# Sixteen conditioning units of a two-block transformer moved from TensorE's products to multiply-adds on GpSimd

## The reference

```python
c_act = jax.nn.silu(c)                                   # (1, 1024)
for l in range(2):
    if l == 1:
        kv_shift, kv_scale = split(c_act @ kv_ada_w + kv_ada_b, 2)
    sh1, sc1, g1, sh2, sc2, g2 = split(c_act @ ada_w[l] + ada_b[l], 6)
    h = x * (1 + sc1) + sh1
    out = conv_module(h) if l == 0 else moba_attention(h @ w_q, k, v) @ w_o
    x = layer_norm(ALPHA * x + (1 + g1) * out, ...)
    h = x * (1 + sc2) + sh2
    f = swiglu(h, ffn_w13, ffn_w2) if l == 0 else moe_swiglu(h, ...)
    x = layer_norm(ALPHA * x + (1 + g2) * f, ...)
return second_block(x, ...)
```

## Time and profile before

| | us |
|---|---|
| runs, median of 3 | 2249.0 (2247.69 to 2250.14) |
| profiled execution | 2244.34 |
| its span | 2242.6 |
| TensorE busy in the span | 2175.9 |
| VectorE, ScalarE, GpSimd busy | 1711.5, 1362.7, 94.1 |
| feed-forward stage, 190.0 to 388.1 | 198.1 |
| ln1, 388.1 to 404.5 | 16.4 |
| k, v, q, 404.5 to 472.5 | 68.0 |
| attention, 472.5 to 521.5 | 49.0 |

### The profile page before, as it was taken

How to read it: one execution, slowest core, us unless ns; L and a number is a source line. 1 busy time by engine, 2 the same in 40 slices (tenths; PEclk the granted TensorE clock), 3 DMA queues, 4 the chain that set the end, 5 groups by cost and what they waited for, 6 DMA issues and landing times.

```text
span 2242.6 us, 35191 instructions
## 1 busy us (share of the span) xinstructions
PE 2175.9 (97%) x14098; PEld 1846.7 (82%) x14098; DVE 1711.5 (76%) x1688; ACT 1362.7 (61%) x1266; POOL 94.1 (4%) x166
## 2 busy tenths in 40 slices
PE   7999999998999999999999999999999999999998
PEld 4767999876888888888888888888998898888887
DVE  3876445646888888888888898886677478999966
ACT  3145334545777777777777777774555335777744
POOL 7500000001000000000000000000000000000000
PEclk8999999999999999999999999999999999999999
DMA  9685754674599999999999999996951152999960
GB/s 356 237 286 183 261 188 161 233 251 163 211 350 393 385 371 370 372 370 372 368 374 369 372 365 377 370 372 182 194 163 39 34 176 76 363 368 366 370 225 20
DMA packets 294171, 619.76 MB, mean 276 GB/s; under 512 B 24845, under 2 KB 102488, under 8 KB 294008
## 3 DMA queue, kind: packets, MB, share of 16 engines
q1 hardware_dynamic: 293200, 617.18, 77.9%
q10 hardware_dynamic: 808, 0.30, 0.1%
HBM read 615.30 MB, written 1.05 MB: 275 GB/s over the span
## 4 chain that ended last, share of the span: by engine, by line
PE 90%; DVE 5%; ACT 2%; DMA 2%; issue 1%; SPq 1%; DVEq 0%; ACTq 0%
PE bank L1325 11%; PE bank L1326 11%; PE bank L1327 11%; PE bank L2291 6%; PE bank L2293 6%; PE bank L2292 6%; PE bank L1367 6%; PE bank L1366 6%; PE bank L1368 6%; PE bank L2352 2%; PE bank L1341 1%; PE bank L1402 1%; PE bank L1299 1%; PE bank L635 1%; PE bank L2491 1%; PE bank L2410 1%
## 5 line engine op out<-in xcount | busy, mean ns | idle before, releaser
L1456 DVE TENSOR_TENSOR ring_lo<-ring_raw,ring_hi 128x2048 fp32r<-128x2048 f32 x432 | 988.4, 2291 | 132.6 <-ACT ring_hi L1449 132.0
L1449 ACT ACTIVATE ring_hi<-ring_raw 128x2048 fp32r<-128x2048 f32 x432 | 828.1, 1920 | 294.4 <-PE bank L1327 174.6
L1325 PE MATMUL bank<-ring_hi,xg_hi 128*128 128x512 f32 x1152 | 456.8, 397 | 1.9 <-DVE ring_lo L1456 1.9
L1326 PE MATMUL bank<-ring_hi,xg_lo 128*128 128x512 f32 x1152 | 449.6, 390 | 0.0
L1327 PE MATMUL bank<-ring_lo,xg_hi 128*128 128x512 f32 x1152 | 449.4, 390 | 0.0
L507 DVE TENSOR_TENSOR ring_lo<-ring_raw,ring_hi 128x2048 fp32r<-128x2048 f32 x95 | 215.8, 2280 | 119.2 <-ACT ring_hi L489 106.0
L2291 PE MATMUL bank<-Hh,ring_hi 128*128 128x256 f32 x936 | 266.4, 285 | 2.7 <-DVE ring_lo L507 1.4
L2293 PE MATMUL bank<-Hh,ring_lo 128*128 128x256 f32 x936 | 264.9, 283 | 0.0
L2292 PE MATMUL bank<-Hl,ring_hi 128*128 128x256 f32 x904 | 255.8, 283 | 0.0
L1327 PEld LDWEIGHTS bank<-ring_lo,xg_hi 128*128 128x128 f32 x1152 | 216.2, 188 | 46.8
L1325 PEld LDWEIGHTS bank<-ring_hi,xg_hi 128*128 128x128 f32 x1152 | 216.4, 188 | 46.6 <-issue 2.7
(11 more groups left out here) (542 smaller groups left out, 2730.2 us busy)
## 6 DMA issues: line engine op xcount, KB each, us to landing
ring_raw<-in_moe_w SPq DMA_DIRECT2D x672, 512.0 KB, 5.2
ring_raw<-in_ada_w SPq DMA_DIRECT2D x96, 512.0 KB, 5.2
ring_raw<-in_ffn_w SPq DMA_DIRECT2D x66, 512.0 KB, 4.8
ring_raw<-in_exp_gate SPq DMA_DIRECT2D x64, 512.0 KB, 5.2
ring_raw<-in_exp_up SPq DMA_DIRECT2D x64, 512.0 KB, 5.3
ring_raw<-in_exp_down SPq DMA_DIRECT2D x64, 512.0 KB, 5.3
ring_raw<-in_w_in SPq DMA_DIRECT2D x42, 512.0 KB, 7.4
ring_raw<-in_conv_in_w SPq DMA_DIRECT2D x16, 512.0 KB, 9.3
```

The costliest lines, as they stand in the source:

```text
L1325: mm(o, xg_hi[:, g, kk, :], wh(k), start=(kk == 0), stop=False)
L1326: mm(o, xg_lo[:, g, kk, :], wh(k), start=False, stop=False)
L1449: nc.scalar.activation(ring_hi[:, at % SPLIT, :], ring_raw[:, n % RAW, :], ACT.Copy)\
L1456: nc.vector.tensor_tensor(ring_lo[:, at % SPLIT, :], ring_raw[:, n % RAW, :], ring_hi[:, at % SPLIT, :].bitcast(F32), ALU.subtract).then_i ...
```

## The change

Four of the six vectors of the second layer (1.0, 1.2, 1.3, 1.4; sixteen units) are no longer multiplied by TensorE. GpSimd multiplies each raw unit, in its slot, by the value of `c_act` that belongs to each partition (`TENSOR_SCALAR`), and adds the result to a sum of 128x1024 in SBUF (`TENSOR_TENSOR`). TensorE then adds over the partitions and turns in one step: `turn_sum`, eight products of a 128x128 block of the sum with a column of ones. The row copies on ScalarE go. The sixteen units are spread over the list: one behind each ffn2, k and v unit until there are no more, which is one behind each of ffn2 0 to 10, k 0 to 3 and v 0. SyncE waits for GpSimd's mark "added n" before it reuses such a slot, and the count `unit_done` leaves them out. In attention, `turn_sum` stands at heads 1, 5 and 9 and three keep-warm products at the odd heads 7, 11, 13 and 15. The calls of `split_hi` and `split_lo` are put in terms of split units (`two_ahead`); those of the code quoted above stay.

```diff
-    late = [("ada", 1, j) for j in range(4)]
+    SUMMED = (0, 2, 3, 4)
+    summed_parts = [("ada", 1, 4 * v + i) for v in SUMMED for i in range(4)]
+    late = list(summed_parts)
+
+    def summed_part():
+        if late:
+            ada_part(1, late.pop(0)[2], A["ada_w"][1])
 
     def down(j):
         add(("ffn2", j), w2, 0, D, 2, r0=256 * j)
-        for _ in range(3):
-            if late:
-                key = late.pop(0)
-                ada_part(1, key[2], A["ada_w"][1])
+        summed_part()
...
     for j in range(4):
         add(("k", j), A["w_kv"], 256 * j)
+        summed_part()
     for j in range(4):
         add(("v", j), A["w_kv"], D + 512 * (j // 2), 512, 4, r0=512 * (j % 2))
+        summed_part()
     for j in range(4):
         add(("q", j), A["w_q"][0], 256 * j)
-    ada(1, 2, 5)
+    assert not late
...
+                elif m in on_pool:
+                    sp.eng.wait_ge(*T.at("added %d" % m))
                 else:
                     sp.eng.wait_ge(T.sem("unit_done"), done_at(m))
...
+            pool.eng.wait_ge(*T.at("ccol"))
+            pool.eng.wait_ge(*T.at("mm mean ln0"))
+            for _, l, j in summed_parts:
+                n = at_unit[("ada", l, j)]
+                w, _ = weights(n)
+                total = sum_of[j // 4]
+                landed(pool, n)
+                for k in range(2):
+                    kk = 2 * (j % 4) + k
+                    eng.tensor_scalar(w[:, k, :] if kk else total, w[:, k, :], cpad[:, kk, 0:1], None, ALU.mult)\
+                        .then_inc(pool.tick(f"added {n}"), 1)
+                for k in range(2):
+                    if 2 * (j % 4) + k:
+                        pool.eng.wait_ge(*pool.own())
+                        eng.tensor_tensor(total, total, w[:, k, :], ALU.add).then_inc(pool.tick(f"added {n}"), 1)
+                T.mark(f"sum {l} {j // 4}", *pool.last)
...
-                for _ in range(3):
-                    if late:
-                        adaptive(1, late.pop(0), turned)
-                        if not late:
-                            turn_row(turned)
+                if j == 5:
+                    turn_sum(1, 0)
+
+            def turn_sum(l, v):
+
+                o = turned(l, v)
+                pe.eng.wait_ge(*T.at(f"sum {l} {v}"))
+                for k in range(KT):
+                    last = mm(o[:, k:k + 1], sum_of[v][:, k * P:(k + 1) * P], ones[:, 0:1], start=True, stop=True)
+                last.then_inc(pe.tick(f"mm turn {l} {v}"), 1)
...
             def between(i):
-                if i < 12:
-                    adaptive(1, 8 + i, None)
-                if i in (5, 9, 13):
-                    turn_row(turned)
+                if i in (1, 5, 9):
+                    turn_sum(1, 2 + i // 4)
+                elif i >= 6 and i % 2 and i < HEADS:
+                    keep_busy(3, "C")
```

More of the change, by code:

```diff
@@ L253, in block_pair @@
                          at_unit["ada", 0, 6]: at_unit["ada", 0, 6], at_unit["ada", 0, 7]: at_unit["ada", 0, 7]}
+    on_pool = [at_unit[key] for key in summed_parts]
     def done_at(n):
-        return done_out_of_order.get(n, n + 1)
+        return done_out_of_order.get(n, n + 1 - sum(i <= n for i in on_pool))
     split_before = [0]
@@ L459, in block_pair @@
         p_in = uF[:, 0:512].rearrange("p (a d) -> p a d", a=TT)
+        sum_of = dict(zip(SUMMED, (uF[:, 0:D], uF[:, D:2 * D], flat(convd)[:, 0:D], flat(convd)[:, D:2 * D])))
         cpad = scr[:, 0, :].rearrange("p (k m) -> p k m", k=KT)
@@ L512, in block_pair @@
         after_split = lambda i: split_units[i]
+        two_ahead = lambda key: split_units[split_before[at_unit[key]] + 2]
+        last_q = at_unit[("q", 3)]
         def attention(pe, name, heads, Q, K, V, between=None):
@@ L1312, in finish @@
                 last.then_inc(T.sem("unit_done"), 1)
-                T.mark(label, "unit_done", U + i + 1)
+                T.mark(label, "unit_done", done_at(U + i))
             def up(n, what, o, extra=None):
@@ L1447, in moe_hi @@
                 landed(act, n)
-                act.eng.wait_ge(T.sem("unit_done"), after_split(at - SPLIT) + 1)
+                act.eng.wait_ge(T.sem("unit_done"), done_at(after_split(at - SPLIT)))
                 nc.scalar.activation(ring_hi[:, at % SPLIT, :], ring_raw[:, n % RAW, :], ACT.Copy)\
@@ L2295, in columns @@
                 for i in jobs:
-                    T.mark("mm " + i, "unit_done", n + 1)
+                    T.mark("mm " + i, "unit_done", done_at(n))
             def columns_by_block(named, Xh, Xl, fresh):
@@ L2334, in rows_of @@
                 for t in range(TT):
-                    T.mark(f"mm {job}.{t}", "unit_done", n + 1)
+                    T.mark(f"mm {job}.{t}", "unit_done", done_at(n))
             to_turn = []
@@ L2512, in _ @@
             acc = []
-            late = list(range(4))
             def turned(l, v):
@@ L2666, in projected @@
                     unit_end(last, n)
-                T.mark(f"mm pp.{i}", "unit_done", n + 1)
+                T.mark(f"mm pp.{i}", "unit_done", done_at(n))
             def first_projected():
@@ L2841, in _ @@
             act.stage = "ffn"
-            late = list(range(4))
             for j in range(NP + 1):
                 if j < NP:
-                    split_hi(act, at_unit[("ffn b", j)] + 2)
+                    split_hi(act, two_ahead(("ffn b", j)) if j + 1 < NP else at_unit[("ffn2", j)])
                     act.eng.wait_ge(*T.at(f"mm ffn a {j}"))
@@ L2856, in _ @@
                     run(Gh[:, g:g + 2, :], tC[:, g:g + 2, :], ACT.Copy).then_inc(act.tick(f"fh {j}"), 1)
-                if j:
-                    for _ in range(3):
-                        if late:
-                            late.pop(0)
-                            if not late:
-                                row_out(1, 0)
             split_hi(act, at_unit[("k", 1)])
@@ L2881, in _ @@
             for j in range(4):
-                split_hi(act, at_unit[("k", j)] + 2)
+                split_hi(act, two_ahead(("k", j)))
                 act.eng.wait_ge(*T.at(f"mm k {j}"))
@@ L2890, in _ @@
             for j in range(4):
-                split_hi(act, at_unit[("v", j)] + 2)
+                split_hi(act, two_ahead(("v", j)))
                 c = j // 2
@@ L2899, in _ @@
             for j in range(4):
-                split_hi(act, at_unit[("q", j)] + 2)
+                split_hi(act, min(at_unit[("q", j)] + 2, last_q))
                 act.eng.wait_ge(*T.at(f"mm q {j}"))
@@ L2905, in between @@
             def between(i):
-                if i % 4 == 3 and i < 12:
-                    row_out(1, 2 + i // 4, 0)
                 if i == 16:
@@ L3258, in _ @@
                 if j < NP:
-                    split_lo(dve, at_unit[("ffn b", j)] + 2)
-                    if j == 3:
+                    split_lo(dve, two_ahead(("ffn b", j)) if j + 1 < NP else at_unit[("ffn2", j)])
+                    if j == 7:
                         biased("turn 1 0", [(1, 0)])
@@ L3292, in _ @@
                 for j in range(4):
-                    split_lo(dve, at_unit[(key, j)] + (2 if key == "q" and j == 3 else 2))
+                    split_lo(dve, min(two_ahead((key, j)), last_q))
             def between(i):
-                if i in (6, 10, 14):
-                    v = 2 + (i - 6) // 4
+                if i in (2, 6, 10):
+                    v = 2 + i // 4
                     biased(f"turn 1 {v}", [(1, v)])
```

2 lines of the change are left out of this document (1 added, 1 removed).

## The result

| | before | after |
|---|---|---|
| median of the runs | 2249.57 us (4 runs) | 2273.16 us (4 runs, 2268.91 to 2276.42) |
| ratio | | 1.0104, 95% interval 1.0088 to 1.0121 |
| profiled execution | 2244.3 us | 2271.4 us |

The account below looks back on a forecast made before the run. TensorE, busy 97% of the span, was taken as the bound. Savings of -7.0, late load +9.2, GpSimd beside VectorE +9 and clock +3 gave +14.2 us: 2258.5 profiled, 2263 as median, range 2250 to 2279.

Parts of the forecast that it names:

- taken off the feed-forward: Feed-forward on TensorE: four conditioning units go (5.4 us), one turning of the summed vector comes; net -3.5 us.
- taken off the attention: Attention on TensorE: twelve units and three turnings go; pairs of heads take 5.0 to 5.5 us; -3.5 us, bounds 0 and -4.
- load of k 1 late: Before ln1: k 1's load waits for ada 1.4's slot, its split holds up gating and residual; +9.2 us, bounds 8 and 11.
- GpSimd beside VectorE: ln1 and k to q: VectorE instructions with two SBUF inputs wait for running GpSimd ones; +9 us, bounds 0 and 23.4.
- clock: ln1, perhaps first of k: TensorE idle from about 390 to 399, clock likely falls to half; +3 us, bounds 0 and 6.7.
- the exemption: ln1 to k: about a third of VectorE's time has one SBUF input, taken as not held; 6 of 19.2 us counted.
- the prediction's own last sign of being wrong: New profile, GpSimd: the prediction is wrong if GpSimd's instructions are several times their estimate (6.4 us a unit).
- The late load alone: ln1 and k: GpSimd's work falls between VectorE's instructions and the clock holds; +2.2 us, 2251; chance 0.12.
- no late load: ScalarE between 382.6 and 388.3: the wait on k 1 is shorter than read, so faster; -7.0 us, 2242; chance 0.10.
- Full exclusion: ln1 and k: every GpSimd microsecond of the last four units delays VectorE on the path; +28.6 us, 2278; chance 0.08.
- GpSimd as the bound: Feed-forward: beyond 18 us a unit the ring starves it; at 21 us, 33 more, 2296; chance 0.03.

## Why the prediction was right, and where its sizes were off

| step | forecast | measured | from |
|---|---|---|---|
| taken off the feed-forward | -3.5 | -3.1 | stages; -3.3 alone (four units) |
| taken off the attention | -3.5 | -1.8 | stages |
| load of k 1 late | +9.2 | +10.9 | split moved behind the gating |
| GpSimd beside VectorE | +9 | +12.3 | 3.1 left in ln1 (1.6 of it unexplained), 9.2 not busy in k to q |
| clock | +3 | +5.0 | TensorE's longer busy time in k to q |
| sum | +14.2 | +23.3 | |

**Feed-forward.** The turning took its 1.84 for 1.8. The stage gave 0.4 less than forecast, 0.2 with the four units alone; no run divides that further.

**Attention.** The pairs take the 5.3 us that were forecast, once the clock is whole. The error is that the first ones ran partly at 1.2 GHz: of the four stretches below, which are the half-clock ones after 390 in the changed kernel, the last is theirs.

```profile
394.80:405.00 10.20, 2.77 (x7) 2.27 (x8) 9.14 (x12) 3.85 (x9) 10.12 (x4) 0.50 0.11 45
435.80:439.20 3.40, 3.40 (x18) 3.40 (x17) 3.36 (x3) 3.40 (x3) 3.32 (x2) 0.51 0.92 326
446.00:452.80 6.80, 5.82 (x27) 5.85 (x28) 6.70 (x6) 3.37 (x4) 6.72 (x2) 0.50 0.66 215
504.00:510.80 6.80, 5.44 (x26) 4.60 (x26) 3.80 (x15) 3.37 (x14) 0.00 (x0) 0.50 0.00 0
```

What brings the clock down in the attention stayed open: kernels with fewer units there had such stretches in six profiles (0.87 to 0.96) and none in two, of which one has the very attention of one of the six; and the kernel with idle TENSOR_TENSOR, with all units in place, had one too (0.97). Extra products did not cure it.

**The late load.** The mechanism is shown by the moved split. The landing was forecast at 393.7, and the split that waited for it began at 393.83. With GpSimd's work small the late load cost 9.7, near the 9.2 of the forecast. Most of what was 1.7 short is thus what only came beside GpSimd's full work, 1.2 us: the chain that the load made late then ran into GpSimd's additions, which held VectorE's folds.

**GpSimd beside VectorE.** The step that failed is the price and the exemption. The multiplication was put at the 0.95 us of a MEMSET of as many columns; undisturbed it takes 2.84 (ln1's row at 400.62), three times that, and the addition, put at 2.26, takes 2.34. Five units, not the four that I counted, were left when the feed-forward ended (7 and 12 instructions in the windows). Together they brought 57.5 us of GpSimd's work (20.74 and 36.74) for my 23.4. And I exempted a third of VectorE's work for reading one tensor only, which the two kernels with idle instructions refute for TENSOR_SCALAR. A longer presence and no exemption should have given much more than 12.3: the 57.5 us cost 17.3 with the clock. What the sum left out works the other way: multiplications, ten of the nineteen instructions here, hold VectorE for a fraction of their length. An estimate from the two kernels with idle instructions, 5.2 us for 14 multiplications and 19.4 for 14 additions, gives 10 x 0.37 + 9 x 1.39 = 16.2 us, near the 17.3. So it is partly luck that the term came out at +9 beside +12.3: 2.5 times the work, at a smaller price for each microsecond of it. By the prediction's own last sign of being wrong, GpSimd's instructions at several times their estimate, the multiplication was wrong (3.0 times, 3.8 in the mean); a whole unit took 2.1 times its estimate.

Why was TENSOR_SCALAR held with one tensor in? The kernel before has it, with two scalars of a partition, in three forms:

```profile
L3086 DVE TENSOR_SCALAR tD<-tA,fold 128x256 f32<-128x256 f32 x16 | 5.9, 410 | 0.3
L3389 DVE TENSOR_SCALAR tA<-tA,scales 128x512 f32<-128x512 f32 x2 | 1.0, 543 | 0.0
L3402 DVE TENSOR_SCALAR xT<-bank,cols 128x256 f32<-128x256 f32 x4 | 2.1, 539 | 0.4 <-PE bank L2609 0.4
```

From SBUF, 256 columns more cost 133 ns, 0.52 ns a column; VectorE's TENSOR_TENSOR of 512 and of 2048 columns, 692 and 2291 ns, are 1.04 ns a column apart. And the same 256 columns from PSUM (`bank`) take 129 ns longer. So the SBUF form runs at double speed, behind a longer fixed part.

The Trainium skill (SBUF — State Buffer, Who interferes with whom) has the exclusion for two SBUF inputs, and the rows bear it out: 0.17 became 2.30 us, 0.69 became 2.65. It exempts a VectorE instruction with at most one SBUF input only outside its two-port modes (2x_2P and 4x_2P), and names TENSOR_SCALAR among those that can enter one; the 0.52 ns a column and the 409 ns that became some 2350 agree with it. The prediction took the exemption without that condition. How long VectorE is held depends on what GpSimd does: up to the whole of an addition, about 0.8 us at most of a multiplication of 2.84.

**The clock.** Right that it would fall in ln1 (0.83), wrong where it costs: 1.1 us there, as the kernel kept warm shows, and 5.0 in k to q, in stretches that follow TensorE's waits for late splits. These vanish with GpSimd's work (clock 1.00 in k to q), so they belong to the step above as its second half.

**Rivals.** The late load alone (2251) falls with GpSimd's work made small, which takes 14.2 us off k to q; no late load (2242) falls with the moved split and the 10.20 us wait. Full exclusion (2278) is nearer in time than its 0.08, 5 us off against 10 for the forecast, but not in mechanism: with the 57.5 us that really came it would give some 2312. GpSimd as the bound did not happen here, at 13.4 us a unit against 18; with two units in a row it did for a stretch.

## What to carry to other kernels

A unit in a shared ring is given back by whoever used it last: moved to a slower engine or behind another block, it delays the load six places on, and if an engine's program still holds that load's split ahead of work that was ready, all of it waits. GpSimd's work is free where VectorE has slack and TensorE does not wait for it, and costs where VectorE's short instructions form the chain (19.4 us for 35.9 us of additions, 5.2 for 48.3 us of multiplications); place it by that, one unit per period, not wherever TensorE is relieved. Here the same idea, twelve units kept within the feed-forward, turned +1.0% into -0.3%.

## What the runs showed of the hardware that I had not expected

- GpSimd's TENSOR_SCALAR of 128x1024 fp32 with a scalar of a partition takes 2.84 us alone, longer than its TENSOR_TENSOR of that size (2.34), and three times its MEMSET.
- GpSimd's TENSOR_TENSOR holds VectorE for its whole length, its TENSOR_SCALAR for about 0.8 us at most at a time: 14 of the first cost 19.4 us, 14 of the second 5.2.
- VectorE's TENSOR_SCALAR with one tensor from SBUF and two scalars of a partition is held too; it takes 0.52 ns a column there, half of TENSOR_TENSOR's 1.04.
- VectorE's TENSOR_TENSOR with one input from PSUM was not held. The four below take 2.48 us together (0.60 from start to start, 683 ns each) while GpSimd was at an addition until 409.17. In the kernel with idle additions, whose first began at 394.86, and in the kernel before they take the same 2.48.

```profile
407.34 2.48 DVE L3157 TENSOR_TENSOR tA<-tA,bank 128x512 f32<-128x512 f32 x4 [2.07 <-PE bank L2430]
```
```profile
406.80 2.37 POOL L2224 TENSOR_TENSOR convd<-convd,ring_raw 128x1024 f32<-128x1024 f32 x1
```
```profile
394.74 2.48 DVE L3142 TENSOR_TENSOR tA<-tA,bank 128x512 f32<-128x512 f32 x4 [1.69 <-PE bank L2410]
```
